# Inverse roots of the group and layer norms: from eight VectorE steps on 256 replicated columns to two columns, a power on GpSimd and a product with ones

## The reference, cut to what matters

```python
y = xf * lax.rsqrt(jnp.mean(xf * xf, axis=-1, keepdims=True) + EPS)
```

```python
mu = jnp.mean(xf, axis=-1, keepdims=True)
var = jnp.mean(jnp.square(xf - mu), axis=-1, keepdims=True)
y = (xf - mu) * lax.rsqrt(var + EPS)
y = jax.nn.silu(y * norm_g + norm_b)
c_out = y @ w_o
```

## Time and profile before

| | |
|---|---|
| median of three runs | 2044.1 us |
| the profiled execution, its own time | 2042.34 us |
| its span (first to last instruction) | 2040.5 us |
| mean granted TensorE clock | 0.992 of full speed |
| PE busy | 1979.1 us, 97% |
| DVE busy | 1657.4 us, 81% |
| ACT busy | 1114.2 us, 55% |
| POOL busy | 142.7 us, 7% |
| DMA | 404.64 MB, mean 198 GB/s |

### The profile page before, as it was taken

The page is one execution under the profiler, slowest core; times in us unless marked ns, Lnnn a source line. Parts: engine busy times, 40 slices in busy tenths (PEclk is TensorE's granted clock), DMA queues, the critical chain, the costliest instruction groups (busy, mean ns, idle before and its releaser), DMA issues.

```text
span 2040.5 us, 29620 instructions
## 1 busy us (share of the span) xinstructions
PE 1979.1 (97%) x11323; PEld 1694.8 (83%) x11323; DVE 1657.4 (81%) x2464; ACT 1114.2 (55%) x1535; POOL 142.7 (7%) x258
## 2 busy tenths in 40 slices
PE   7999989999999999999999999999999999998998
PEld 6877889988878778888778888888888887787886
DVE  5877779888989987988987888877888889876665
ACT  5555454455674365577347645454665773365553
POOL 4000000000004000002300000000000013000000
PEclk9999999999999999999999999999999999998999
DMA  8635476677656656556656676777766566554653
GB/s 268 202 123 193 153 221 207 196 234 236 206 169 195 201 171 214 183 156 190 211 168 203 200 247 229 239 244 227 249 221 194 176 190 203 186 187 126 213 177 123
DMA packets 196716, 404.64 MB, mean 198 GB/s; under 512 B 15767, under 2 KB 18067, under 8 KB 196576
## 3 DMA queue, kind: packets, MB, share of 16 engines
q1 hardware_dynamic: 187888, 387.50, 59.8%
q0 software_dynamic: 8688, 15.25, 2.5%
HBM read 396.74 MB, written 1.10 MB: 195 GB/s over the span
## 4 chain that ended last, share of the span: by engine, by line
PE 72%; issue 14%; DVE 9%; ACT 5%; DMA 1%; POOL 0%; DVEq 0%; POOLq 0%; ACTq 0%
PE gps L1229 13%; PE gps L1231 13%; PE gps L1230 13%; PE gps L1253 6%; PE gps L1236 4%; PE gps L1237 4%; PE gps L1238 4%; PE gps L1255 3%; DVE wlo L2163 2%; PE gps L1213 2%; PE aps L1165 2%; PE aps L1131 2%; ACT whi L1634 1%; PE aps L1005 1%; PE aps L1118 1%
## 5 line engine op out<-in xcount | busy, mean ns | idle before, releaser
L2163 DVE TENSOR_TENSOR wlo<-raw,whi 128x1024 fp32r<-128x1024 f32 (+1 forms) x648 | 760.6, 1186 | 238.9 <-ACT whi L1634 236.1
L1634 ACT ACTIVATE whi<-raw 128x1024 fp32r<-128x1024 f32 (+1 forms) x648 | 660.6, 1027 | 529.1 <-PE gps L1231 377.8
L1229 PE MATMUL gps<-whi,both 128*128 128x512 f32 x1624 | 649.1, 400 | 6.8 <-DVE wlo L2163 6.6
L1231 PE MATMUL gps<-whi,both 128*128 128x512 f32 x1624 | 634.1, 390 | 0.0
L1230 PE MATMUL gps<-wlo,both 128*128 128x512 f32 x1624 | 633.9, 390 | 0.0
L1229 PEld LDWEIGHTS gps<-whi,both 128*128 128x128 f32 x1624 | 305.6, 188 | 79.9 <-DVE wlo L2163 11.6
L1231 PEld LDWEIGHTS gps<-whi,both 128*128 128x128 f32 x1624 | 305.5, 188 | 65.4
L1230 PEld LDWEIGHTS gps<-wlo,both 128*128 128x128 f32 x1624 | 305.8, 188 | 60.5
L1236 PE MATMUL gps<-both,whi 128*128 128x256 f32 x960 | 276.1, 288 | 1.5 <-DVE wlo L2163 1.5
L1237 PE MATMUL gps<-both,whi 128*128 128x256 f32 x960 | 271.7, 283 | 0.0
L1238 PE MATMUL gps<-both,wlo 128*128 128x256 f32 x960 | 271.6, 283 | 0.0
(11 more groups left out here) (314 smaller groups left out, 1759.9 us busy)
## 6 DMA issues: line engine op xcount, KB each, us to landing
raw<-w_in SPq DMA_DIRECT2D x232, 512.0 KB, 4.3
raw<-w_ff SPq DMA_DIRECT2D x192, 512.0 KB, 4.6
raw<-ada_wT SPq DMA_DIRECT2D x96, 512.0 KB, 4.4
raw<-w_attn_o SPq DMA_DIRECT2D x24, 512.0 KB, 4.3
raw<-w_gmlp_o SPq DMA_DIRECT2D x24, 512.0 KB, 3.8
raw<-w_conv_o SPq DMA_DIRECT2D x24, 512.0 KB, 3.8
raw<-w_out SPq DMA_DIRECT2D x24, 512.0 KB, 4.7
raw<-w_gate SPq DMA_DIRECT2D x20, 512.0 KB, 4.9
```

What stands on the lines that cost most here:

```text
L1229: mm(om, ah, whi[:, q, i, :], start=first, stop=False)
L1231: t = mm(om, al, whi[:, q, i, :], start=False, stop=last)
L1634: A_(part(whi, jb, q), raw_part(jb, q), ACT.Copy).then_inc(hi_done[q], 1)
L2163: tt(part(wlo, jb, q), raw_part(jb, q), f32(part(whi, jb, q)), ALU.subtract).then_inc(lo_done[q], 1)
```

## The change

The sums are made the other way round, with the squares as the weights and two columns of `ones` as the moving operand. That gives the statistic of a position on its own partition, one column for each half of the 256 positions. DVE adds EPS to these 128x2 values, POOL raises them to -0.5, and DVE multiplies the identity with each of the two columns, which gives two diagonal matrices of 128x128 (the factor D = 1024 cancels the 1/1024 in `ones`). PE multiplies `ones` with the diagonals, which puts the inverse root of each position in every partition of bank 2, and DVE scales the tiles from there. The five uses of `rsqrt` on 256 columns go; a semaphore `root_step` counts the four steps of each norm.

Places: "ynD" is a new step at unit 3 of the same job as "ynM", LATE, and "ynB" a new one at (`j_km0`, 0) and (`j_oa[0]`, 1). "ynL" moves one unit earlier at (`j_km0`, 2) and one later at (`j_oa[0]`, 1). For the layer norms "ln_dg" is new at (`gates[4]`, 2), LATE, and "ln_bc" at (`gates[4]`, 3).

```diff
-    put(j_km0, 2, "ynL", slot=2, half=0)
+        put(hosts[2], 3, "ynD", half=group)
+    put(j_km0, 0, "ynB", half=0)
+    put(j_km0, 1, "ynL", slot=2, half=0)
...
-    put(j_oa[0], 1, "ynL", slot=2, half=1)
+    put(j_oa[0], 1, "ynB", half=1)
+    put(j_oa[0], 2, "ynL", slot=2, half=1)
...
         put(gates[4], 2, "ln_norm", of=lm)
+        put(gates[4], 2, "ln_dg", of=lm)
+        put(gates[4], 3, "ln_bc", of=lm)
...
             elif k == "ynM":
-                use(p, (2,), ("yn_ms", None, 0, p.half + 1))
+                use(p, (2,), ("root_step", None, 0, 4 * p.half + 1))
+            elif k == "ynB":
+                use(p, (2,), ("yn_y", None, 0, p.half + 1))
...
+            def root(k):
+                pool.wait_ge(sem["root_step"], 4 * k + 1)
+                nc.gpsimd.tensor_tensor(st[:, 15, 2:4], st[:, 15, 0:2], half_power[:], ALU.pow).then_inc(sem["root_step"], 1)
...
-                for k in range(4):
-                    t = mm(aps[:, 2, 0:S], ones[:], AB[:, k * S:(k + 1) * S], start=k == 0, stop=k == 3)
+                for m in range(2):
+                    for k in range(4):
+                        t = mm(aps[:, 2, 2 * m:2 * m + 2], AB[:, k * S + m * P:k * S + m * P + P], ones[:, 0:2],
+                               start=m == 0 and k == 0, stop=m == 1 and k == 3, skip_group_check=True)
                 t.then_inc(sem["yn_ss"], 1)
+
+            def spread(diagonals):
+                for m in range(2):
+                    t = mm(aps[:, 2, m * P:m * P + P], ones[:], diagonals[:, m * P:m * P + P], start=m == 0, stop=m == 1,
+                           skip_group_check=True)
+                return t
+
+            def yn_spread(p):
+                free(p)
+                pe.wait_ge(sem["root_step"], 4 * p.half + 3)
+                spread(GB).then_inc(sem["root_step"], 1)
...
+            def ln_spread(p):
+                pe.wait_ge(sem["root_step"], 4 * p.of.n + 11)
+                spread(PTb).then_inc(sem["root_step"], 1)
...
+            def diagonals(to):
+                for m in range(2):
+                    t = ts(to[:, m * P:m * P + P], ident[:], st[:, 15, 2 + m:3 + m], float(D), ALU.mult, ALU.mult)
+                return t
+
+            def yn_mean(p):
+                dve.wait_ge(sem["yn_ss"], p.half + 1)
+                ts(st[:, 15, 0:2], aps[:, 2, 0:4:2], 2.0, EPS, ALU.mult, ALU.add).then_inc(sem["root_step"], 1)
...
             def yn_scale(p):
...
-                rsqrt(rs, x, t_)
+                dve.wait_ge(sem["root_step"], 4 * p.half + 4)
                 for k in range(4 * p.half, 4 * p.half + 4):
                     y = RB[:, k * S:(k + 1) * S]
-                    t = stt(y, y, C1[:, 16 + k:17 + k], rs, ALU.mult, ALU.mult)
+                    t = stt(y, y, C1[:, 16 + k:17 + k], aps[:, 2, 0:S], ALU.mult, ALU.mult)
...
             def ln_norm(p):
                 wait(dve, ev("ln_vs", p.of))
-                x, r, t_ = PTb[:, 0:S], PTb[:, S:2 * S], PTb[:, 2 * S:3 * S]
-                link(ts(x, aps[:, 2, S:2 * S], CUBIC, EPS * CUBIC, ALU.mult, ALU.add))
-                rsqrt(r, x, t_)
+                ts(st[:, 15, 0:2], aps[:, 2, S:S + 4:2], EPS, None, ALU.add).then_inc(sem["root_step"], 1)
+
+            def ln_diagonals(p):
+                dve.wait_ge(sem["root_step"], 4 * p.of.n + 10)
+                diagonals(PTb).then_inc(sem["root_step"], 1)
+
+            def ln_scale(p):
+                dve.wait_ge(sem["root_step"], 4 * p.of.n + 12)
+                r = aps[:, 2, 0:S]
...
-            LATE = ("conv", "ynM", "rq", "rk", "gv_rms", "gv_norm", "final")
+            LATE = ("conv", "ynM", "ynD", "ln_dg", "rq", "rk", "gv_rms", "gv_norm", "final")
```

More of the change, by code:

```diff
@@ L651 @@
 pn_ss pn_e pn_w po_e po_w pn_xn pn_xa t_pe t_hi t_lo
-ba_s ba_sb ba_nm ba_p ba_pn ba_tp ba_pt ba_pv ba_y yn_sq yn_ss yn_ms yn_y yn_hi yn_lo
+ba_s ba_sb ba_nm ba_p ba_pn ba_tp ba_pt ba_pv ba_y yn_sq yn_ss root_step yn_y yn_hi yn_lo
 ma_s ma_nm ma_p ma_pn ma_tp ma_pt ma_pv ma_hi ma_lo
@@ L949, in at_inverse, with yn_root, ln_root @@
                 nc.gpsimd.tensor_tensor(den[:, d0 + 6:d0 + 8], den[:, d0 + 4:d0 + 6], minus_one[:], ALU.pow).then_inc(sem["at_r"], 1)
-            stages = dict(atR=at_inverse, pn_stat=pn_root, po=po_root, wsT=ws_load, rep=copies, toep=toep, ba=ba, ctx_load=ctx_load, modT=mod_t, gb=gb, tab=tab)
+            def root(k):
+                pool.wait_ge(sem["root_step"], 4 * k + 1)
+                nc.gpsimd.tensor_tensor(st[:, 15, 2:4], st[:, 15, 0:2], half_power[:], ALU.pow).then_inc(sem["root_step"], 1)
+            def yn_root(p):
+                root(p.half)
+            def ln_root(p):
+                root(p.of.n + 2)
+            stages = dict(ynM=yn_root, ln_norm=ln_root, atR=at_inverse, pn_stat=pn_root, po=po_root, wsT=ws_load, rep=copies, toep=toep, ba=ba, ctx_load=ctx_load, modT=mod_t, gb=gb, tab=tab)
             for jb in jobs:
@@ L1194, in ln_norm @@
             def ln_norm(p):
-                ln_total(p, 1).then_inc(sem["ln_vs"], 1)
+                wait(pe, ev("ln_pc", p.of, 2, 2))
+                for m in range(2):
+                    t = mm(aps[:, 2, S + 2 * m:S + 2 * m + 2], PTb[:, 3 * S + m * P:3 * S + m * P + P], ones[:, 0:2], start=m == 0,
+                           stop=m == 1, skip_group_check=True)
+                t.then_inc(sem["ln_vs"], 1)
+            def ln_spread(p):
+                pe.wait_ge(sem["root_step"], 4 * p.of.n + 11)
+                spread(PTb).then_inc(sem["root_step"], 1)
             stages = dict(pp=pp, pp2=pp2, toep=toep, T=T, ba=ba, baT=baT, baV=baV, ynM=yn_sum, ma=ma, maT=maT, maV=maV,
                           tq=tq, tk=tk, at=at, atT=atT, atV=atV, spatial=spatial, wsT=ws_t, modT=mod_t,
-                          ck=ck, ln_mu=ln_mu, ln_mean=ln_mean, ln_var=ln_var, ln_norm=ln_norm)
+                          ck=ck, ln_mu=ln_mu, ln_mean=ln_mean, ln_var=ln_var, ln_norm=ln_norm, ln_bc=ln_spread, ynB=yn_spread)
             def unit(jb, q):
@@ L1829, in ba, with yn_diagonals @@
                     t.then_inc(sem["ba_pn"], 1)
-            def yn_scale(p):
[L1832 to L1837, removed]
-                rsqrt(rs, x, t_)
+            def diagonals(to):
+                for m in range(2):
+                    t = ts(to[:, m * P:m * P + P], ident[:], st[:, 15, 2 + m:3 + m], float(D), ALU.mult, ALU.mult)
[3 more added lines that the diff above has]
+                ts(st[:, 15, 0:2], aps[:, 2, 0:4:2], 2.0, EPS, ALU.mult, ALU.add).then_inc(sem["root_step"], 1)
+            def yn_diagonals(p):
+                dve.wait_ge(sem["tp_st"], 16)
+                dve.wait_ge(sem["root_step"], 4 * p.half + 2)
+                diagonals(GB).then_inc(sem["root_step"], 1)
+            def yn_scale(p):
+                dve.wait_ge(sem["root_step"], 4 * p.half + 4)
                 for k in range(4 * p.half, 4 * p.half + 4):
                     y = RB[:, k * S:(k + 1) * S]
-                    t = stt(y, y, C1[:, 16 + k:17 + k], rs, ALU.mult, ALU.mult)
+                    t = stt(y, y, C1[:, 16 + k:17 + k], aps[:, 2, 0:S], ALU.mult, ALU.mult)
                 t.then_inc(sem["yn_y"], 1)
@@ L2006, in ln_lo @@
                     ALU.subtract).then_inc(sem["ln_lo"], 1)
-            stages = dict(pn_stat=pn_stat, final=final, po=po, T=T, pp_c=pp_c, ada=ada, ada2=ada, pp=pp, pp2=pp2, toep=toep, ba=ba, ynM=yn_scale, ynL=yn_lo, ma=ma,
+            stages = dict(pn_stat=pn_stat, final=final, po=po, T=T, pp_c=pp_c, ada=ada, ada2=ada, pp=pp, pp2=pp2, toep=toep, ba=ba, ynM=yn_mean, ynD=yn_diagonals, ynB=yn_scale, ynL=yn_lo, ma=ma,
                           maV=maV, mod=mod, rope=rope, rq=rq, rk=rk, at=at, atL=atL, gv_rms=gv_rms, gv_norm=gv_norm, spatial=spatial,
-                          conv=conv, ln_mean=ln_mean, ln_norm=ln_norm, ln_mul=ln_mul, ln_lo=ln_lo)
-            LATE = ("conv", "ynM", "rq", "rk", "gv_rms", "gv_norm", "final")
+                          conv=conv, ln_mean=ln_mean, ln_norm=ln_norm, ln_dg=ln_diagonals, ln_bc=ln_scale, ln_mul=ln_mul, ln_lo=ln_lo)
+            LATE = ("conv", "ynM", "ynD", "ln_dg", "rq", "rk", "gv_rms", "gv_norm", "final")
             def res_add(jb, g):
```

## The result

The changed kernel takes 2057.45 us (median of 4 runs, 2054.78 to 2059.33) against 2044.11 us before: the ratio is 1.0065 with a 95% interval of 1.0053 to 1.0078, so it is 13.3 us slower. Measured again later, the ratio is 1.0052 (1.0040 to 1.0065), or 11.9 us by the medians. One execution of the kernel with the group norms' product one unit later took 2837.56 us at a mean granted clock of 0.653 and is left out; all others of this document are in the fast state. The profiled execution took 2056.6 us with a span of 2054.8 us, 14.3 us more than the profiled one before.

A forecast was written before the change was run, and what follows sets the result against it. PE, busy 97% of the span, was taken to bound the kernel. Terms 9.0 + 1.4 - 1.9 + 1.7 gave +10.2 us; against the median of 2044.1 us the forecast was 2054.3 us, range 2047.5 to 2061.0.

The forecast's parts named there:

- The new wait of PE: At each layer norm PE waits for diagonals written behind a split that PE itself releases: +3.0 us each, +9.0 for three.
- The first group norm: PE starts `j_km0` 5.4 us late, but the old waits of 3.48 + 0.54 us are covered: net +1.4 us.
- The second group norm: PE idles 2.5 us ahead of `j_oa[0]` unit 1; net -0.2 us, -1.9 together with an old low clock gone.
- Clock: Of four new PE idle times of 2.5 to 2.8 us, likeliest one lowers the clock: +1.7 us.
- The narrow sums: PE's sums go from 22 to 44 two-column records at 0.11 us: zero change, between 4.7 us gained and 3.6 lost.
- The power on POOL: From DVE's 128x2 step over POOL's power to DVE's next takes 1.00 us; hidden at the layer norms by ACT's split.
- Busy times: DVE's busy time falls by some 17 us over the kernel, PE's rises by 2 to 3.
- ACT's wait at the layer norms: ACT's wait for the first scaled half at each layer norm stays as long as before the change.
- A: PE regains two thirds of the layer norms' 9.0 us at later waits, no clock lost: 2046.6 us, chance 0.12.
- B: Faster: at the norms the diagonals are ready when PE comes; -8.0 us, 2036.1 us, chance 0.06.
- C: Two-column records on PE take 0.19 us and all four idle times lower the clock: +18.9, 2063.0 us, chance 0.07.
- D: The wide `rsqrt` steps remain somewhere, so the change does not do what it says; given no chance.

The follow-up runs named there:

- the layer-norm kernel: The changed kernel with the group norms put back as they were before; ratio 1.0065 to the kernel before, 2057.3 us.
- the doubled power: POOL's power done twice at each layer norm: in the changed kernel ratio 1.0075; with diagonals ahead of the split and group norms' product one unit later, 0.9996.
- the group norms alone: The changed kernel with the group norms' product one unit later and the layer norms of the kernel before; ratio 0.9969, 2037.5 against 2043.4 us.

## Why the prediction was right, and where it was off

2054.3 us was predicted, range 2047.5 to 2061.0, and 2057.45 was measured. By the steps:

- **The new wait of PE, the main term.** Right in place, cause and size. Idle times of 2.8, 4.8 and 2.4 us were forecast and 2.86, 5.06 and 2.56 came. Taking "ln_dg" ahead of the split cut it to 0.63 us, which shows the cause at the layer norms; at the group norms moving the product shows it. A layer norm was put at +3.0 and measured +2.5 to +2.8 without clock; between 0.6 and 1.0 us came back instead of 0.5.
- **The first group norm.** +1.4 was forecast, +3.9 came. The old waits of 3.48 + 0.54 us are covered as forecast, but 0.71 us of new waiting for DVE's softmax appears at 126.48, ahead of a product of scores and values. And "the stretch at 1.2 GHz stays, only earlier" was wrong by 1.7 us: behind the longer idle time the low clock lasted twice as long (0.66 over 10 us, 3.4 us), here and in each of the four other profiled executions with an idle time of 5.06 us there.
- **The second group norm.** -1.9 forecast, -2.0 measured, with the idle time and the full clock that were forecast.
- **Clock.** I counted one low clock in the three idle times at the layer norms and the one at the second group norm; the profiled execution had two, its repeat one, and the layer-norm kernel's three. In the profiled execution (+14.3 us) this term is 1.7 us short and the first group norm 2.5; the 1.1 us near 266 stand in no term, and the three layer norms were put 1.1 us too high. So a part of the misses cancelled.
- **The narrow sums.** Zero change, as forecast: sixteen records take 1.84 us, eight wide ones took 1.89. Single records of the trace start 0.112 us apart (only the second starts 0.025 us behind the first), so the lower bound (time follows the columns) is refuted, and so is the upper one of 0.19 us. The Trainium skill (TensorE: Matmul & The Clock Gate, section on LDWEIGHTS) gives 107 ns for a weight load of 128 columns. The spacing in this trace agrees with that to 5 ns, though the profile's own records of these loads are 0.19 us long.
- **The power on POOL.** 1.06 us from mean to diagonals against 1.00, hidden at the layer norms as forecast; the doubled power shows both cases. The bias load behind it left at 107.18, as forecast, and PE waited for nothing from it.
- **Busy times.** DVE's fell by 15.2 us and not by 17, because the 4.0 us of a norm were elapsed time with small gaps in it. PE's rose by 5.2 us and not by 2 to 3, and records that run at the low clock are longer.
- **ACT's wait at the layer norms** was to stay as it was, and grew from 3.23 to 4.10 us at the first. The product there took 1.11 us at the low clock instead of 0.5.
- **Rivals.** A (delays given back): 1 us or less of each comes back. The waits for a split that A counted on, away from the norms, were 0.47 and 1.41 us, less than the 2.7 us in the prediction, and both are there after the change. B (faster) did not come; its deciding point of 0.5 us of idle time was too strict, since the group norms alone gain 5.9 us with idle times of 1.3 and 1.2 us ahead of their products. C was half right, in the clock. D: DVE lost 15.2 us of work, so the change does what it says.

## What to carry to other kernels

Before moving work from a half-idle engine to a chain over three engines, ask where in each engine's order the links stand: here a step queued behind a conversion that the waiting engine itself releases cost 2.86 us each time, and one word in an ordering tuple took back 7 to 10 us. Give the engine that bounds the kernel its next unit of work between asking and using; here one unit was best at the group norms, and with two the next user of the buffer waited 2.96 us. At the layer norms this was not tried. And count an idle time of that engine with its low clock, not only its length.

## What the runs showed of the hardware

- A product of two columns with full 128x128 float32 weights costs as much as one of 128 columns: its records start 0.112 us apart, like those of the 128-column product with the diagonals at 163.4 (0.112 us); the 128-column transposes in the kernel before start 0.109 us apart.
- An idle time of 2.86 us lowered the clock at two of three layer norms in one execution, at all three in another, and at one in a third; the price was 1.7 or 3.4 us. Over all profiled executions, idle times of 1.3 to 1.4 us left the clock up, and those of 2.2 to 2.9 us went either way. At the same length of waiting, useless products on TensorE kept the clock at 1.00 behind all five norms, and the kernel was 3.7 to 4.8 us faster.
